# Second layer's u product moved onto split weights and a split input

## The reference

```
h = RMSNorm(x); z = h @ w_in[layer]           # 1024 x 1536
ua, ub, vb = z split into three widths of 512
ya = S5 state-space mixer(ua)                 # B u, scan with complex states, C s, GELU, GLU
yb = gelu(ub) * (tril(W_s) @ LayerNorm(gelu(vb)) + b)
x = x + [RMSNorm(ya), RMSNorm(yb)] @ w_out[layer]
x = x + FFN(RMSNorm(x))     # layer 0: dense SwiGLU, hidden width 2752; layer 1: top 2 of 8 experts
y = RMSNorm(x)
```

## Time and profile before

| | |
|---|---|
| median of 3 runs | 842.73 us (841.59 to 844.71) |
| the profiled execution | 845.93 us, its span 844.1 us |
| PE busy | 812.0 us, 96% of the span |
| DVE, ACT, POOL busy | 544.4, 401.9, 215.2 us |
| chain that ended last | PE 76%, DVE 11%, SP's queue 4%, DMA 4% |
| dense products, lines 1351 to 1353, split_u part | 87.4 + 57.2 + 86.9 us |
| granted TensorE clock, mean of the span | 0.986 |
| DMA rate, mean and highest of 40 slices | 238 and 423 GB/s |

### The profile page before, as it was taken

The page is one execution under the profiler, slowest core; times in us unless marked ns, Lnnn a source line. Parts: engine busy times, 40 slices in busy tenths (PEclk is TensorE's granted clock), DMA queues, the critical chain, the costliest instruction groups (busy, mean ns, idle before and its releaser), DMA issues.

```text
span 844.1 us, 13719 instructions
## 1 busy us (share of the span) xinstructions
PE 812.0 (96%) x5048; PEld 630.9 (75%) x5048; DVE 544.4 (64%) x1006; ACT 401.9 (48%) x608; POOL 215.2 (25%) x182
## 2 busy tenths in 40 slices
PE   9999899999999999999999999999999998999985
PEld 7488679999999999668777888877866343865322
DVE  8999577466766557569752999699845132863105
ACT  7885455464334440485521696766751022650112
POOL 3811132222444321450211005324123000150003
PEclk9999999999999999999999799999999999999997
DMA  9603625745555521910500798987999999999992
GB/s 293 213 1 115 247 88 172 209 154 162 168 150 153 169 77 54 286 68 5 208 1 1 279 419 311 373 283 280 385 364 403 423 419 422 419 414 423 420 410 83
DMA packets 89554, 201.02 MB, mean 238 GB/s; under 512 B 24225, under 2 KB 48049, under 8 KB 89489
## 3 DMA queue, kind: packets, MB, share of 16 engines
q1 hardware_dynamic: 88560, 199.12, 64.8%
q10 hardware_dynamic: 576, 0.59, 0.2%
q0 software_dynamic: 352, 0.44, 0.2%
HBM read 198.51 MB, written 1.61 MB: 237 GB/s over the span
## 4 chain that ended last, share of the span: by engine, by line
PE 76%; DVE 11%; SPq 4%; DMA 4%; issue 2%; ACT 2%; POOL 1%; DVEq 0%; POOLq 0%; ACTq 0%
PE ps L1698 8%; PE ps L1352 8%; PE ps L1351 8%; PE ps L1353 8%; PE ps L1555 6%; PE ps L1445 4%; PE ps L1361 4%; SPq L789 4%; PE ps L1682 3%; PE ps L1683 3%; PE ps L1685 3%; PE ps L1825 2%; PE ps L1826 2%; PE ps L1829 2%; DMA wraw_d<-in_moe_w_gate 2%
## 5 line engine op out<-in xcount | busy, mean ns | idle before, releaser
L1351 PE MATMUL ps<-Md,split_u 128*128 128x288 f32 x296 | 87.4, 295 | 0.0
L1353 PE MATMUL ps<-Md,split_u 128*128 128x288 f32 x296 | 86.9, 294 | 0.0
L1882 DVE TENSOR_TENSOR xb<-xb,ps 128x288 f32<-128x288 f32 x80 | 33.3, 450 | 60.2 <-PE ps L1555 26.5
L847 POOL TENSOR_TENSOR wrnd_g<-wraw_g,wrnd_g 128x1024 fp32r<-128x1024 f32 (+1 forms) x6 | 21.1, 3512 | 179.0 <-ACT wrnd_g L1028 179.0
L1022 ACT ACTIVATE split_u<-raw 128x1024 fp32r<-128x1024 f32 (+1 forms) x39 | 40.3, 1034 | 44.3 <-PE ps L1353 44.3
L1352 PE MATMUL ps<-hbr,split_u 128*128 128x288 f32 x192 | 57.2, 298 | 0.0
L1882 DVE TENSOR_TENSOR wrnd_d<-wraw_d,wrnd_d 128x1376 fp32r<-128x1376 f32 (+2 forms) x20 | 34.0, 1731 | 35.2 <-ACT wrnd_d L1028 35.2
L1882 DVE TENSOR_TENSOR wrnd_g<-wraw_g,wrnd_g 128x1376 fp32r<-128x1376 f32 (+2 forms) x31 | 48.3, 1577 | 12.4 <-ACT wrnd_g L1028 12.2
L1882 DVE TENSOR_TENSOR wrnd_u<-wraw_u,wrnd_u 128x1376 fp32r<-128x1376 f32 (+2 forms) x34 | 56.3, 1687 | 0.0
L1353 PEld LDWEIGHTS ps<-Md,split_u 128*128 128x128 f32 x296 | 55.7, 188 | 0.0
L1351 PEld LDWEIGHTS ps<-Md,split_u 128*128 128x128 f32 x296 | 55.6, 188 | 0.1
(11 more groups left out here) (476 smaller groups left out, 2172.3 us busy)
## 6 DMA issues: line engine op xcount, KB each, us to landing
wraw_g<-in_moe_w_gate SPq DMA_DIRECT2D x31, 688.0 KB, 10.7
wraw_u<-in_moe_w_up SPq DMA_DIRECT2D x29, 688.0 KB, 17.5
wraw_d<-in_moe_w_gate SPq DMA_DIRECT2D x22, 688.0 KB, 9.3
wraw_g<-in_moe_w_down SPq DMA_DIRECT2D x28, 512.0 KB, 15.8
wraw_u<-in_moe_w_down SPq DMA_DIRECT2D x28, 512.0 KB, 13.3
raw<-in_ffn_w_gate SPq DMA_DIRECT2D x21, 512.0 KB, 4.5
raw<-in_ffn_w_up SPq DMA_DIRECT2D x21, 512.0 KB, 4.7
raw<-in_ffn_w_down SPq DMA_DIRECT2D x21, 512.0 KB, 4.0
```

The source lines that it names most:

```text
L1351: pe.matmul(out, w_hi, x_hi, start=start, stop=False)
L1353: return pe.matmul(out, w_lo, x_hi, start=False, stop=stop)
L1882: return dve.tensor_tensor(o, a, b, op)
```

## The change

Layer 1's u weights become chunks 66 to 69 (`ALL` = 70) of the dense ring: loaded, rounded and subtracted like the others, all four subtractions by DVE. The input is split too: ACT writes `h_h`, DVE `h_l1` (`mix_low`). PE makes 96 rounded products instead of 32 float32 ones. What now lies where raw buffers, split chunks and halves are still in use moves or waits: w_in for v and ub get new places in G; C, h0 and POOL's clearing of the bias wait for all of u; the constants, ln and wst for the first two of the four chunks; `scaled_u` for all four banks; and the mean is taken later in PE's order.

```diff
 DENSE = 2 * HALF_CHUNKS
+U_CHUNKS = 4
+ALL = DENSE + U_CHUNKS
 def by_pool(n):
-    return (n + SHIFT) % NSPLIT in POOL_SLOTS
+    return n < DENSE and (n + SHIFT) % NSPLIT in POOL_SLOTS
...
+        w_b = [w_in[:, :, MIX:2 * MIX], G[:, KT * MIX:].rearrange("p (k f) -> p k f", f=2 * MIX)[:, :, 0:MIX]]
+        w_v = [w_in[:, :, 2 * MIX:IN_W], G[:, KT * MIX:].rearrange("p (k f) -> p k f", f=2 * MIX)[:, :, MIX:2 * MIX]]
...
+        mag_tabs = [t.rearrange("p (n c) -> p n c", n=NP) for t in (U[:, 9216:10240], G[:, 0:1024])]
...
+        h_l1 = split_u[:, 400:400 + KT * T].rearrange("p (k t) -> p k t", t=T)
...
         def load_in(l):
                 if l:
-                    for n in (DENSE - 2, DENSE - 1):
-                        wait_low(sp, n)
+                    wait_low(sp, ALL - 1)
                     pools = [n for n in range(DENSE) if by_pool(n)]
                     wait_low(sp, pools[-1])
-                if l:
-                    piece(0, 0, 4, 0)
                     sp.wait_ge(chunk_used, DENSE)
                     sp.wait_ge(rot_ready, 3)
                     sp.wait_ge(bp_ready, 2)
+                    sp.dma_start(w_v[1], src[:, :, 2 * MIX:IN_W]).then_inc(w_in_in[2], 16)
...
+                if l == 0:
+                    for r in range(2):
+                        sp.dma_start(CPX[:, r, :, 0, :], c_d[l, :, r]).then_inc(c_in, 16)
+                    piece(2, 0, KT, 2 * MIX)
+                else:
+                    sp.wait_ge(chunk_used, DENSE + 2)
                 sp.dma_start(D[:, 9216:10240], ln_d[l]).then_inc(mix_in, 16)
                 sp.dma_start(wst, wst_d[l]).then_inc(mix_in, 16)
...
                 if l:
+                    sp.wait_ge(ua_mm, 2 * MT)
+                    for r in range(2):
+                        sp.dma_start(CPX[:, r, :, 0, :], c_d[l, :, r]).then_inc(c_in, 16)
                     sp.wait_ge(sv_ready, 1)
                     sp.wait_ge(ms_mm, 5)
                 for r in range(2):
                     sp.dma_start(S[:, r, :, 0:NCS], h0_d[l, :, r]).then_inc(mix_in, 16)
...
         @block.gpsimd
+                    pool.wait_ge(ms_mm, 5)
+                    pool.memset(S[:, :, :, NCS:NCS + 1], 0.0).then_inc(set_ready, 1)
...
+                    pool.wait_ge(ua_mm, 2 * MT)
...
         @block.scalar
-                    squares(x, sq0[1], 0, lambda k: act.wait_ge(xadd, X_DENSE[1] + k + 1))
+                    act.wait_ge(chunk_used, DENSE - 1)
+                    for k in range(KT):
+                        act.wait_ge(h_ready, 24 + k + 1)
+                        act.activation(h_h[:, k, :], h[:, k, :], ACT.Copy).then_inc(hh_ready, 1)
+                        act.activation(sq0[1][:, k, :], x[:, k, :], ACT.Square).then_inc(sq_ready, 1)
                     mirrored_rotation(1)
...
-                        if n < DENSE:
+                        if n < ALL:
                             high(n)
...
         @block.tensor
                 def u_product(q, k):
+                    n = ALL - 2 - 2 * (k // 4) + q // 2
+                    if k % 4 == 0 and q % 2 == 0:
+                        wait_low(pe, n)
+                    at = (k % 4) * 2 * P + (q % 2) * P
+                    w_hi, w_lo = [w[:, at:at + P] for w in split_slot(n)]
+                    mm = split_mm(bank(q), w_hi, w_lo, h_h[:, k, :], h_l1[:, k, :], k == 0, k == KT - 1)
+                    if k == 3 and q % 2:
+                        mm.then_inc(chunk_used, 1)
+                    return mm
                 for k in range(4):
-                    pe.wait_ge(h_ready, 24 * l + k + 1)
+                    if l:
+                        pe.wait_ge(hl_ready, KT + k + 1)
...
                         if l and k == 0 and q:
                             pe.wait_ge(h_ready, 24 + q + 1)
...
-                else:
-                    pe.wait_ge(xadd, X_DENSE[1] + 8)
-                    mean_pair(sq0[1], KT - 1, 7, 32, 5)
+                for k in (4, 5) if l else ():
+                    pe.wait_ge(hl_ready, KT + k + 1)
+                    for q in range(MT):
+                        u_product(q, k)
                 for q in range(MT):
-                    for k in range(4, KT):
+                    for k in range(6 if l else 4, KT):
...
+                    if l and q == 0:
+                        pe.wait_ge(xadd, X_DENSE[1] + 8)
+                        mean_pair(sq0[1], KT - 1, 7, 32, 5)
...
         @block.vector
+                    dve.wait_ge(chunk_used, DENSE + 2)
                     dve.tensor_copy(sv(0, 30), sv_ahead(0, 30)).then_inc(sv_ready, 1)
...
                     for q in range(MT):
-                        dve.wait_ge(ua_mm, 4 * l + q + 1)
+                        dve.wait_ge(ua_mm, 2 * MT if l else q + 1)
...
+                def mix_low(k):
+                    dve.wait_ge(hh_ready, KT + k + 1)
+                    tt(h_l1[:, k, :], h[:, k, :], h_h[:, k, :].bitcast(F32), ALU.subtract).then_inc(hl_ready, 1)
...
                                         gained(h[:, m, :], 1, "norm_mix", m)
+                                        if m:
+                                            mix_low(m - 1)
+                                if hf:
+                                    mix_low(KT - 1)
-                        if n < DENSE and not by_pool(n):
+                        if n < ALL and not by_pool(n):
                             low(n)
```

More of the change, by code:

```diff
@@ L340, in build @@
         sq2 = M[:, 0:KT * T].rearrange("p (k t) -> p k t", t=T)
-        sq0 = [M[:, c:c + KT * T].rearrange("p (k t) -> p k t", t=T) for c in (6176, 6336)]
+        sq0 = [t.rearrange("p (k t) -> p k t", t=T) for t in (M[:, 6176:6176 + KT * T], M[:, 3872:3872 + KT * T])]
         hx = M[:, 2304:2304 + KT * T].rearrange("p (k t) -> p k t", t=T)
@@ L407, in dense_chunk @@
         def dense_chunk(n):
+            if n >= DENSE:
+                return "u", (n - DENSE) % 2, (ALL - 1 - n) // 2, P, 4 * 2 * P
             hf, c = divmod(n, HALF_CHUNKS)
@@ L690, in load_in @@
                     load_x(1)
-                piece(1, 4, KT, 0)
+                    piece(1, 4, KT, 0)
                 sp.dma_start(sb_raw, sbias_d[l].rearrange("(h t) -> h t", h=NH)[:, LS:]).then_inc(bias_in, 16)
@@ L695, in load_in @@
                     sp.dma_start(misc[:, 0:72], misc_d).then_inc(const_in, 16)
-                for r in range(2):
-                    sp.dma_start(CPX[:, r, :, 0, :], c_d[l, :, r]).then_inc(c_in, 16)
-                piece(2, 0, KT, 2 * MIX)
+                if l == 0:
[4 more added lines that the diff above has]
+                    sp.wait_ge(chunk_used, DENSE + 2)
                 sp.dma_start(D[:, 9216:10240], ln_d[l]).then_inc(mix_in, 16)
@@ L707, in load_in @@
                     sp.dma_start(S[:, r, :, 0:NCS], h0_d[l, :, r]).then_inc(mix_in, 16)
-                piece(3, 0, KT, MIX)
+                sp.dma_start(w_b[l], src[:, :, MIX:2 * MIX]).then_inc(w_in_in[3], 16)
                 sp.dma_start(glu, glu_d[l]).then_inc(glu_in, 16)
@@ L731, in _ @@
                 if l == 0:
-                    for n in range(DENSE):
+                    for n in range(ALL):
                         if n >= NRAW:
@@ L738, in _ @@
                         kind, a, kh, r, w = dense_chunk(n)
-                        hf = n // HALF_CHUNKS
+                        hf = min(n // HALF_CHUNKS, 1)
                         f0 = HALF_AT[hf]
-                        if kind == "down":
+                        if kind == "u":
+                            src = w_in_d[1].rearrange("(k p) f -> p k f", p=P)[:, 4 * kh:4 * kh + 4, 2 * P * a:2 * P * (a + 1)]
+                            dst = raw_slot(n)[:, 0:w].rearrange("p (k f) -> p k f", k=4)
+                        elif kind == "down":
                             if n == DENSE - 1:
@@ L891, in _ @@
                     pool.wait_ge(chunk_used, DENSE)
-                pool.memset(S[:, :, :, NCS:NCS + 1], 0.0).then_inc(set_ready, 1)
-                if l:
+                if l == 0:
+                    pool.memset(S[:, :, :, NCS:NCS + 1], 0.0).then_inc(set_ready, 1)
+                else:
                     for k in range(1, KT - 1):
                         add_blocks(sq0[1], k, KT, 24)
+                    pool.wait_ge(ms_mm, 5)
+                    pool.memset(S[:, :, :, NCS:NCS + 1], 0.0).then_inc(set_ready, 1)
                 if l:
@@ L1359, in u_product @@
                 def u_product(q, k):
-                    return pe.matmul(bank(q), w_in[:, k, q * P:(q + 1) * P], h[:, k, :],
-                                     start=(k == 0), stop=(k == KT - 1), skip_group_check=True)
-                for k in range(4):
-                    pe.wait_ge(h_ready, 24 * l + k + 1)
[L1366 to L1369, removed]
+                    if l == 0:
+                        return pe.matmul(bank(q), w_in[:, k, q * P:(q + 1) * P], h[:, k, :],
+                                         start=(k == 0), stop=(k == KT - 1), skip_group_check=True)
+                    n = ALL - 2 - 2 * (k // 4) + q // 2
```

(37 more changed lines are left out.)

3 lines of the change are left out of this document (1 added, 2 removed).

## The result

The changed kernel takes 845.38 us (median of 20 runs) where the kernel before takes 842.51 (20 runs beside it): ratio 1.0040, 95% interval 1.0028 to 1.0053, or 2.4 to 4.5 us slower. I had forecast 846.0, +3.3. The profiled execution is 849.68 us with a span of 847.8; part of its distance from the profile of before (3.7 us of span) lies behind the stretch that changed: from the first product behind the second mean after y to the end of the kernel the profiles of this case took between 411.4 and 417.0 us (415.8 before, 417.0 changed).

What follows compares the result with a forecast made beforehand. PE was taken to bound the kernel, with ACT 1.97 us behind. +2.5 us at the transposes' copies (PE's savings included) and +0.8 at the scan gave +3.3: 842.7 + 3.3 = 846.0 us, range 842.0 to 850.5.

Steps and rivals of the forecast that it cites:

- PE's products: u on PE: 15.7 us of float32 products replaced by 12.7 us of split products, saving 3.0 us if PE never waits.
- DVE's backlog: End of the dense ring: the new subtractions delay DVE's pieces of B, so the first add to x comes 1.0 us later.
- Start of u: PE's first block of u waits for the input's halves: 2.5 us lost, leaving 1.3 of the 3.0 us saved.
- C: After u: C lands 5.7 us after its late issue, ACT's run starts 4.5 later; less 1.97 slack, +2.5 at the transposes' copies.
- rival D: Clock falls to half after PE's new waits at u's start and in the transposes: up to 5 us, 851 us; chance 0.10.
- h0: Issued behind C, landing 7 us after issue at 361.5; the delay to v's statistics is covered by 2 us on ACT.
- Rival C: Late C or h0 holds ACT or DVE's statistics, hence ACT's third copy of S and PE's ub: 848.5 to 851.5; chance 0.18.
- Scan beside POOL: POOL's powers of C run into DVE's scan chain, which PE's third y needs: +0.8 us, from 0 to 2.5.

Runs made afterwards that it cites:

- b_late_c: Kernel before, with only layer 1's load of C issued after u's last product, h0 and w_in for ub behind it: 844.80 us against 842.81, ratio 1.0039.
- a_stage_c: Changed kernel with C loaded during u into free columns of G and copied into place by ACT after u: 843.21 us against 842.81, ratio 1.0009.
- a_fill4: Changed kernel with four products of ones in PE's wait in layer 1's B transposes: 844.55 us against 842.57, ratio 1.0020.
- a_b_early: Changed kernel with the last five pieces of B at chunks 62, 64, 65, 66 and 67 instead of 66 to 70: 844.41 us against 842.81, ratio 1.0029.
- a_order: Changed kernel with banks 2 and 3 after both blocks of banks 0 and 1 in PE's start of u: 845.40 us against 842.35, ratio 1.0029.
- a_fill: Changed kernel with eight products of ones in PE's wait in layer 1's B transposes: 849.52 us against 842.35, ratio 1.0089.
- a_fill_late_w: Changed kernel with eight products of ones in the B transposes and layer 1's w_out issued only after y: 846.12 us against 842.57, ratio 1.0050.
- a_all: Changed kernel with C staged early, B's last five pieces earlier and u's first two blocks re-ordered: 841.76 us against 842.81, ratio 0.9988.
- a_best: Changed kernel with C staged early, B's pieces earlier, u's first blocks re-ordered and PE's bank waits on the adds: 841.03 us against 842.35, ratio 0.9983.

## Why the prediction came out right, step by step

- **PE's products.** 3.0 us saved but for waits: the split products of u come at 0.132 us (24 starts from 339.10 to 342.13), 0.133 predicted.
- **DVE's backlog.** First add 1.26 us after the last down chunk's start, 0.46 before: 0.8 late, 1.0 predicted.
- **Start of u.** Waits of 1.02 and 1.23, together 2.25, where I had 2.5. Net gain to r 0.65 us; predicted 1.0 (1.3 less the 0.3 for the reciprocal, measured 0.20).
- **C.** The mechanism is shown from both sides, by b_late_c and a_stage_c. The size was off: both halves landed 5.1 us after the first issue and not 5.7 (3.0 and 4.6 us each after its own issue, where it was 5.6 and 6.8 with the weights in front), ACT's run 4.0 late and not 4.5, its copies of the transposes at 372.35, which is 1.86 late against the dense stage and not 2.5. At ub that is +1.66 (2.30 longer from the transposes in a_fill4, less 0.64 by which PE reaches them sooner). The Trainium skill's fit (DMA: Bandwidth & Descriptors, Anatomy of one DMA) gave an estimate of 3.2 us for this load; the page has that fit for transfers issued by GpSimd, and these are issued by SP. The measured 5.1, with runs of 128 bytes in two transfers, decides.
- **The clock.** I had it as rival D, chance 0.10, at up to 5 us. It did fall, for 3.4 us, and cost 1.55 up to ub, of which 0.8 is left at the third bank of y (a_fill4). The forecast's total holds because this term took the place of what C was short of and of the wait for the scan; that was luck in the sizes.
- **h0.** Landed 4.2 to 4.5 us after issue, no hold: v's statistics ended at 376.7, and DVE then waited 5.8 us for ACT's root. Rival C did not happen.
- **Scan beside POOL.** The collision is there (1.44 for two instructions, 2.23 for a scan that takes 1.20 otherwise), but PE doesn't wait for the chain in the changed kernel: ub to GLU is 36.81 against 36.72, +0.1, where I had +0.8. The reason is the clock and not only the chain's 1.5 us of cover. PE comes to y 1.55 us later by it; where the clock held, PE does wait in front of the third bank of y, 0.82 us in a_fill4, 0.81 in b_late_c and 1.54 in a_b_early. So the term was right in size, and another one hid it. The +0.1 is made of two others that I did not have: PE's wait of 0.71 us for POOL in front of y is gone, and its stop inside y is 0.92 instead of 0.23.

In sum, for the profile: +1.66 for C, +1.55 for the clock up to ub, +0.1 behind ub: 3.3 to GLU. The run times give 2.9 (medians) to 3.4 (ratio).

What stays open: how often the clock falls in runs that were not profiled. Their mean granted clock suggests that it mostly does: its median is 0.990 in the changed kernel and in a_order, whose profiles show the fall, and 0.991 to 0.992 in the kernel before, b_late_c, a_stage_c, a_b_early and a_fill4, whose profiles show none in the transposes; 3.4 us at half take 0.002 from that mean. But single runs of one kernel spread by 0.008 and more. Open as well is why the ratios give more than the profiles' distances to GLU: 0.7 us more in a_stage_c, 1.2 in b_late_c, 1.7 in a_b_early, 2.2 in a_fill and 2.8 in a_fill_late_w, against 0.1 in the changed kernel. The long stretch behind them, with the expert stage, varies by up to 5.6 us from profile to profile. So single steps of a microsecond are shown by the rows and not by the run times.

## What to carry to other kernels

When a product is shortened by keeping its operands in memory that something else was loaded into early, price the load that now comes late, and follow it not to its first reader but to the whole list of the engine that waits for it: half a megabyte that was hidden behind u stood in front of sixteen copies. Before taking work from the busiest engine, read how long the next engine waited for it (here 1.97 us); past that the rest of the saving becomes that engine's idle time. A wait of 2 us on PE may cost more than itself, by what the clock does behind it. And a term that is taken away may uncover the next one: without the clock's fall PE stood at the scan chain.

## What was unexpected of the hardware

- After 2.00 and 2.11 us of PE idleness in the transposes the clock was at half for 3.4 us (the changed kernel, a_order); after 1.68, 1.46 and 0.96 in the same place it was not (b_late_c, a_b_early, a_fill4). Four small products of ones in the gap, 0.9 us, kept it up.
- While w_out was being loaded at up to 426 GB/s, PE stopped with no engine to wait for: 0.23 us before, 0.92 in the changed kernel, a_stage_c and a_order, 0.78 in a_all and a_best, 2.56 with eight more products ahead of it; with four more the stop was 0.70 and stood later, in GLU. Each time PE went on 1.3 to 1.5 us after a 16 KB packet of the `instruction` queue had ended. With w_out issued after y these packets ended 3.3 and 5.0 us earlier and there was no stop. There was none in y either in b_late_c and a_b_early, with w_out moving: PE had just waited 0.81 and 1.54 us for DVE, so that the packet ended 0.75 and 0.01 us after the start of y's third bank, where it ended 1.5 to 1.6 us after it in the six kernels that stopped in that bank.
